# Running the FFN weights' conversion beside the first tile's normalisation, RNN and attention stages in a streaming encoder kernel

## The reference

```
h = rms_norm(x, norm_mix_g)
u, q, k, v, gl = split(h @ w_in)                      # 1024 | 1024 | 256 | 256 | 2048 columns
u = causal_dwconv(u, width 4);  y_rnn = rglru(u)      # gated linear recurrence along the frames
y_attn = banded_window_attention(rms_norm(q), rms_norm(k), v)
g_rnn, g_attn = split(sigmoid(gl + b_gate))
x = x + (g_rnn * (y_rnn @ w_rnn_proj) + g_attn * (y_attn @ w_attn_proj)) @ w_out
h2 = rms_norm(x, norm_ffn_g)
a, b = split(h2 @ w_up)                               # 2 x 2816 columns
x = x + (gelu(causal_dwconv(a, width 3)) * b) @ w_down
```

## Time and profile before

| | us |
|---|---|
| time before, median of 2 runs | 6626.67 |
| the two runs | 6571.98 and 6681.36 |
| the profiled execution's own time | 6345.69 |
| its span (slowest of 8 cores; the others from 6311.2) | 6344.1 |
| TensorE busy | 4429.2 (70% of the span) |
| VectorE, ScalarE, GpSimd busy | 2651.0, 2521.7, 330.4 |

### The profile page before, as it was taken

One profiled execution on the slowest core, in us unless ns is written; L12 is line 12 of the kernel. 1 busy time (PEld: TensorE's weight loads), 2 busy tenths in 40 slices (PEclk: granted clock), 3 DMA queues, 4 the chain that ended last, 5 costly groups with the idle time before them and its releaser, 6 DMA issues.

```text
span 6344.1 us, 81867 instructions; the slowest of 8 cores (6311.2 to 6344.1 us)
## 1 busy us (share of the span) xinstructions
PE 4429.2 (70%) x25752; PEld 2403.9 (38%) x25752; DVE 2651.0 (42%) x5630; ACT 2521.7 (40%) x4313; POOL 330.4 (5%) x446
## 2 busy tenths in 40 slices
PE   0002787878787887878787877778777878787773
PEld 0001343434444443434344443444344444444442
DVE  1002353545445353535454443535353544435353
ACT  0103444353534344444435343444445353434421
POOL 0000000000000000000000000000000000000000
PEclk9999898989898898989898989989898989899885
DMA  6775232323232423333232323233332333232335
GB/s 156 196 196 162 77 112 101 112 102 119 97 120 71 139 98 119 111 111 104 102 113 102 122 77 133 90 126 110 107 107 101 107 105 119 77 133 90 114 127 177
DMA packets 263670, 735.95 MB, mean 116 GB/s; under 512 B 22960, under 2 KB 90224, under 8 KB 263248
## 3 DMA queue, kind: packets, MB, share of 16 engines
q1 hardware_dynamic: 254480, 696.59, 33.9%
q0 software_dynamic: 8768, 34.13, 1.5%
HBM read 663.47 MB, written 67.62 MB: 115 GB/s over the span
## 4 chain that ended last, share of the span: by engine, by line
PE 54%; DMA 15%; DVE 14%; ACT 7%; issue 7%; DVEq 1%; POOL 0%; SPq 0%; ACTq 0%; POOLq 0%
PE psA L482 33%; PE psC L564 13%; DMA wsc<-yr 8%; DVE tl L530 7%; DMA ring<-wsc 6%; DVE tl L533 3%; ACT tl L522 2%; PE psA L752 1%; PE psC L836 1%; PE psB L510 1%; PE psA L818 1%; ACT xn L488 1%; DVE xn L502 1%; DVE yat L851 1%; ACT tl L658 1%
## 5 line engine op out<-in xcount | busy, mean ns | idle before, releaser
L482 PE MATMUL psA<-hTb,ring 128*128 128x512 bf16 (+1 forms) x5984 | 1301.6, 376 | 153.4 <-DVE st L536 108.6
L482 PE MATMUL psA<-hTa,ring 128*128 128x512 bf16 (+1 forms) x4624 | 1076.3, 388 | 244.8 <-DMA ring<-wsc 148.9
L530 DVE SCALAR_TENSOR_TENSOR tl<-psA,prm_s,tl 128x511 f32<-128x511 f32 (+4 forms) x1224 | 845.4, 691 | 882.9 <-ACT tl L522 468.5
L482 PEld LDWEIGHTS psA<-hTb,ring 128*128 128x128 bf16 x5984 | 561.2, 100 | 863.2 <-issue 266.5
L564 PE MATMUL psC<-ring,actb 128*128 128x256 bf16 (+1 forms) x5720 | 732.5, 290 | 209.7 <-DVE xt L571 92.8
L482 PEld LDWEIGHTS psA<-hTa,ring 128*128 128x128 bf16 x4624 | 446.1, 102 | 830.4 <-issue 407.5
L564 PEld LDWEIGHTS psC<-ring,actb 128*128 128x128 bf16 (+1 forms) x5720 | 587.1, 104 | 363.9 <-issue 234.3
L510 PE MATMUL psB<-identb,xn 128*128 128x128 bf16 (+1 forms) x1040 | 103.1, 264 | 746.7 <-DVE xn L502 736.6
L937 ACT ACTIVATE tl<-tl 128x512 f32<-128x512 f32 (+1 forms) x374 | 226.5, 606 | 930.4 <-DVE tl L533 910.5
L522 ACT ACTIVATE tl<-psA,prm_s 128x512 f32<-128x512 f32 (+1 forms) x510 | 378.7, 743 | 348.2 <-PE psA L482 332.7
L908 DVE TENSOR_TENSOR tlb<-psA,tl 128x512 bf16<-128x512 f32 (+1 forms) x136 | 90.0, 662 | 848.0 <-PE psA L482 803.4
(11 more groups left out here) (118 smaller groups left out, 4557.9 us busy)
## 6 DMA issues: line engine op xcount, KB each, us to landing
ring<-wsc SPq DMA_DIRECT2D x1020, 512.0 KB, 4.3
xt<-xp SPq DMA_DIRECT2D x16, 2048.0 KB, 8.8
yp<-xt POOLq DMA_DIRECT2D x16, 2048.0 KB, 8.7
wsc<-yr SPq DMA_DIRECT2D x110, 256.0 KB, 3.6
ring<-wsc SPq DMA_DIRECT2D x68, 384.0 KB, 3.9
actb<-w_in SPq DMA_DIRECT2D x32, 512.0 KB, 5.1
actb<-w_up SPq DMA_DIRECT2D x32, 512.0 KB, 5.0
actb<-w_down SPq DMA_DIRECT2D x22, 512.0 KB, 5.4
```

The costliest lines, as they stand in the source:

```text
L482: P.add("pe", lambda e, kc=kc: e.matmul(out_ap, lhsT=wv[:, kc, col0:col0 + 128], rhs=rhs_t[:, kc, 0:W], start=(kc == 0), stop=(kc == nk - 1)),
L530: P.add("dve", lambda e, c0=c0, L=L, s=s, wj=wj: e.scalar_tensor_tensor(out=acc[:, c0 + s:c0 + L], in0=ps[:, c0:c0 + L - s], scalar=wj, in ...
```

## The change

The 70 chunks of the FFN weights (48 of w_up, 22 of w_down) leave the prepass and become a generator, `prepass_ffn_gen`, with a yield after each chunk. It is stepped by `par` together with the first tile's stage A and front: one chunk per round. These late chunks use three f32 buffers and three bf16 buffers of their own, all in `actb`, because the front writes `yr`; the store of chunk i is recorded after the load of chunk i+2. The remaining 64 chunks keep four buffers of each kind.

The name that a store writes is no longer "wsc" for all, but ("wsc", slot) for each slot it touches, and `load_slot` reads only the name of its slot. A store still waits for the last store to the same slots, which is the one of the row block before: eight chunks back for the first 64 chunks, six back for w_up. For w_down the row block before is the chunk just ahead (`SL_DN + 3 * i + kc // 8`: eight blocks in a row go to the same four slots), so the 22 stores of w_down, but for the first of each eight, still wait for the store ahead of them.

A fence is added behind `mid` of the first tile, ahead of its `ffn_up`, which writes `actb`.

```
--- before.py
+++ after.py
@@ -294,6 +294,8 @@
     NSTG = 4
     stg_f = [actb[:, 4 * i:4 * i + 4, :].rearrange("p a b -> p (a b)").bitcast(F32) for i in range(NSTG)]
     stg_b = [yr[:, 2 * i:2 * i + 2, :].rearrange("p a b -> p (a b)") for i in range(NSTG)]
+    stg_f2 = [actb[:, 4 * i:4 * i + 4, :].rearrange("p a b -> p (a b)").bitcast(F32) for i in range(3)]
+    stg_b2 = [actb[:, 12 + 2 * i:14 + 2 * i, :].rearrange("p a b -> p (a b)") for i in range(3)]
     gstg = tl[:, 2:4, :].rearrange("p a b -> p (a b)")
 
     psA = [P.psum(f"psA{i}", [128, 512], F32) for i in range(4)]
@@ -326,8 +328,8 @@
     d_const = P.dsem("const", serial=True)
     d_x = [P.dsem("x0"), P.dsem("x1")]
     d_ring = [P.dsem(f"ring{i}") for i in range(NRING)]
-    d_stg = [P.dsem(f"stg{i}") for i in range(4)]
-    d_wst = [P.dsem(f"wst{i}") for i in range(4)]
+    d_stg = [P.dsem(f"stg{i}") for i in range(7)]
+    d_wst = [P.dsem(f"wst{i}") for i in range(7)]
     d_y = [P.dsem("y0"), P.dsem("y1")]
     d_fin = P.dsem("fin")
     d_cp = P.dsem("cp")
@@ -406,11 +408,17 @@
     pp = {"i": 0}
     _pre_ok = not (_DBG_STOP is not None and _DBG_STOP <= 1)
 
-    def prepass_chunk(src, kc, c0, ncol, dest_fn, scale):
+    def prepass_chunk(src, kc, c0, ncol, dest_fn, scale, late=False):
         i = pp["i"]
         pp["i"] += 1
-        b = i % NSTG
-        sf, sb = stg_f[b], stg_b[b]
+        if late:
+            b = NSTG + i % 3
+            sf, sb = stg_f2[i % 3], stg_b2[i % 3]
+            depth = 2
+        else:
+            b = i % NSTG
+            sf, sb = stg_f[b], stg_b[b]
+            depth = NSTG - 1
         P.dma(lambda e: e.dma_start(out=sf[:, 0:ncol], in_=src[kc * 128:(kc + 1) * 128, c0:c0 + ncol]), d_stg[b],
               writes=[("stgf", b)])
         eng = ("dve", "act", "pool")[i % 3]
@@ -432,11 +440,11 @@
         dst = wsc[s0:s0 + step * (ng - 1) + 1:step].rearrange("s p c -> p s c")[:, :, kcl * 256:(kcl + 1) * 256]
         pp.setdefault("pend", []).append(
             lambda: P.dma(lambda e: e.dma_start(out=dst, in_=sb[:, 0:ncol].rearrange("p (s c) -> p s c", s=ng)), d_wst[b],
-                          reads=[("stgb", b)], writes=["wsc"]))
-        while len(pp["pend"]) > NSTG - 1:
+                          reads=[("stgb", b)], writes=[("wsc", sl_[0]) for sl_ in slots]))
+        while len(pp["pend"]) > depth:
             pp["pend"].pop(0)()
 
-    for kc in (range(8) if _pre_ok else ()):
+    for kc in range(8):
         g = prmc(P_GM + kc, 1)
         prepass_chunk(w_in_d, kc, 0, 1024, lambda i, kc=kc: (SL_U + i, kc), g)
         prepass_chunk(w_in_d, kc, 1024, 1024, lambda i, kc=kc: (SL_Q + i, kc), g)
@@ -446,13 +454,21 @@
         prepass_chunk(wrp_d, kc, 0, 1024, lambda i, kc=kc: (SL_M + 4 * i + 0, kc), 1.0)
         prepass_chunk(wap_d, kc, 0, 1024, lambda i, kc=kc: (SL_M + 4 * i + 1, kc), 1.0)
         prepass_chunk(wout_d, kc, 0, 1024, lambda i, kc=kc: (SL_O + i, kc), 1.0)
-        gf = prmc(P_GF + kc, 1)
-        for half in range(2):
-            for (c0, ncol, p0) in ((0, 1024, 0), (1024, 1024, 4), (2048, 768, 8)):
-                prepass_chunk(wup_d, kc, half * DFF + c0, ncol,
-                              lambda i, kc=kc, half=half, p0=p0: (SL_UP + 2 * (p0 + i) + half, kc), gf)
-    for kc in (range(NFB) if _pre_ok else ()):
-        prepass_chunk(wdn_d, kc, 0, 1024, lambda i, kc=kc: (SL_DN + 3 * i + kc // 8, kc % 8), 1.0)
+
+    def prepass_ffn_gen():
+        for kc in range(8):
+            gf = prmc(P_GF + kc, 1)
+            for half in range(2):
+                for (c0, ncol, p0) in ((0, 1024, 0), (1024, 1024, 4), (2048, 768, 8)):
+                    prepass_chunk(wup_d, kc, half * DFF + c0, ncol,
+                                  lambda i, kc=kc, half=half, p0=p0: (SL_UP + 2 * (p0 + i) + half, kc), gf, late=True)
+                    yield
+        for kc in range(NFB):
+            prepass_chunk(wdn_d, kc, 0, 1024, lambda i, kc=kc: (SL_DN + 3 * i + kc // 8, kc % 8), 1.0, late=True)
+            yield
+        while pp.get("pend"):
+            pp["pend"].pop(0)()
+        yield
 
     while pp.get("pend"):
         pp["pend"].pop(0)()
@@ -470,7 +486,7 @@
         cnt["ring"] = r + 1
         ring_held[r] = True
         nv = 6 * 256 if (slot >= SL_DN and (slot - SL_DN) % 3 == 2) else 2048
-        P.dma(lambda e: e.dma_start(out=ring[:, r, 0:nv], in_=wsc[slot, :, 0:nv]), d_ring[r], reads=["wsc"],
+        P.dma(lambda e: e.dma_start(out=ring[:, r, 0:nv], in_=wsc[slot, :, 0:nv]), d_ring[r], reads=[("wsc", slot)],
               writes=[("ring", r)])
         return ring[:, r, :].rearrange("p (k c) -> p k c", k=8), ("ring", r), r
 
@@ -962,14 +978,15 @@
         return (ti, b, 32, 32, 1, [(0, 16, 1), (16, 16, 2)], False, True)
 
     load_x(0)
-    run(stageA_gen(*targs(0)))
-    run(front_gen(*targs(0)))
+    run(par([prepass_ffn_gen(), chain([stageA_gen(*targs(0)), front_gen(*targs(0))])]))
     for ti in range(NT + 1):
         b = ti % 2
         if ti + 1 <= NT:
             load_x(ti + 1)
         ta_ = targs(ti)
         mid(*ta_)
+        if ti == 0:
+            P.fence()
         gens = [ffn_up(*ta_[:6])]
         if ti + 1 <= NT:
             gens.append(stageA_gen(*targs(ti + 1)))
```

## The result

The changed kernel takes 6203.1 us (median of 11 runs, 6137.38 to 6450.26). The kernel before takes 6420.84 us in the ten runs that there are of it now (6332.54 to 6681.36). In the comparison the changed kernel's time is 0.9705 of before, 95% interval 0.9657 to 0.9754. That is 3.0% faster, 187 us of the profiled execution's 6345.7 (156 to 218 by the interval). The profiled execution of the changed kernel took 6147.0 us, 198.7 less.

A forecast was written before the change was run, and what follows sets the result against it. The prediction took the prepass stores, which all write one name and wait for each other, to set the pace. Its terms, -51 - 135 + 5 = -181 us, took 6626.7 to 6446 us; range 6285 to 6560.

The forecast's parts named there:

- Step 1: The 64 chunks staying in the prepass: stores with new names stop waiting for each other, 190 us for 241, -51 us.
- the drain: End of the early prepass: its stores must finish before the fence there, 6 us.
- Step 2: The 70 late chunks beside the first tile's stage A and front: 281 us in place of 416, -135 us.
- w_up's 164 us: The 48 late w_up chunks, with frames and ring loads in the queue: 41.9 MB at 256 GB/s, 164 us.
- the locking: Fixed-order engine lists in the late phase: chunk and front work hold each other up, DMA engines idle, +30 us.
- w_down's 73: The 22 late w_down chunks: stores to the same four slots stay chained, 3.3 us each, 73 us.
- a last attention job: End of the late phase: one attention job stands behind the last conversion on ACT, 8 us.
- Step 3: The fence behind the first tile's mid: the first ffn_up ring loads start only then, +5 us.
- The stores' chain is a symptom: Prepass and late w_up: memory gives no more than 197 GB/s however many transfers wait, 6546 us; chance 0.10.
- The queue takes more: Prepass and late w_up: mixed transfers exceed the assumed rate, 44 and 34 us more gain, 6368 us; chance 0.15.
- Half the front unhidden: First tile's front: conversions wait behind front operations, half of 127 us added instead of 30, 6480 us; chance 0.17.
- The closed loop: SP's list in the front: chunk loads, conversions, front operations and matmuls wait in a circle, slower, 6821 us; chance 0.03.

The follow-up runs named there:

- the first combined version: Changed kernel with names per slot and row block, four late buffers of each kind, and names in place of the fence: ratio to before 0.9624.
- its own experiment: Changed kernel with the fence behind mid replaced by names on the six late buffers: 233.9 us from the end of mid to the first tile's store.

## Why the prediction was right and wrong

**The change in time was right, the time was not.** Forecast were 181 us less; the ratio says 187 (156 to 218), the two profiled executions 199. The time of 6446 us and its range (6285 to 6560) missed the 6203.1 that was measured. The step that failed is the one from the profile to the median: "I carry it over as microseconds" from a profiled execution of 6345.7 to a median of two runs, 6626.7. Eight more runs of the kernel before brought that median to 6420.8, 206 us lower, so most of the miss of 243 us is the level of the two runs that were shown. The granted clock named with the result is the likely reason, but the two runs have no times by core, so this is not shown. The text said that nothing in the rows explained why those two lay 226 and 336 us above the profiled execution, and then let the range reach down only part of the way to 6165, the time it had itself worked out for an execution like the profiled one. An unexplained gap in the reference is an unknown like any other, and the range should have held both of its ends.

**Step 1** had the first frames' load near 233 us (190 for the 64 chunks, 6 for the drain). It was at 226.1 on the core of the page before and 211.9 on average. So 64 chunks took some 169 us on average, in place of 236 before (64/134 of 494): 67 us less, where 51 were forecast. The rate at full share, 256 GB/s worked out from share 0.77, was measured as 264 at share 1.06 on the page's core, and as 250 to 297 on the eight cores of the same execution from 40 to 190 us. Here are core 0 and core 5:

```profile
40.00:190.00 150.00, 0.00 (x0) 0.00 (x0) 14.12 (x20) 22.09 (x21) 20.63 (x20) 1.00 1.05 297
...
40.00:190.00 150.00, 0.00 (x0) 0.00 (x0) 11.91 (x17) 18.12 (x17) 17.28 (x17) 1.00 1.04 250
```

The reason given for 190 and not 184, that queued transfers never pack perfectly, has no row behind it: the share is 1.02 to 1.07 on all eight. The part that was taken for granted is right: SP's waits for stores are 1.6 us in the early chunks. The bound from the Trainium skill ("HBM Reference", Specifications: about 358 GB/s per core with a pair streaming) was not reached by loads and stores together: the highest rate of a stretch of 150 us here was 299. Reads alone came close to it for 14 us, and above the 323 that the prediction had as the best of its trace: core 4 of the kernel before had 350 GB/s from 540 to 554 us, at share 0.93.

```profile
40.00:190.00 150.00, 0.00 (x0) 0.00 (x0) 14.12 (x20) 21.06 (x20) 19.63 (x20) 1.00 1.07 289
```

That is the early prepass of the first combined version on the core of its page; its other cores have 287 to 299. That a chain of stores is bound by latency fits what unchaining gave: the same stores, twice as slow each, go at a higher rate once none waits for the one ahead. The Trainium skill ("DMA: Bandwidth & Descriptors", Anatomy of one DMA) puts the fixed part of a DMA issued from GpSimd down mostly to the confirmed write. These stores are issued by SP, and no run here shows what their fixed part consists of.

**Step 2** had 275 us from the first frames to mid's first matmul; on the page's core it is 263.1 (216.8 to 479.9). Of its terms, w_up's 164 us were 173 (217.2 to 389.6), with the locking that was put beside them; w_down's 73 were 68 (389.6 to 458.1); and the 8 for a last attention job were 22, since the last three stores, the 2 MB of frames and mid's first ring loads come after w_down on SP, and PE waits 9.95 us for the last of these. That wait was not in the sum, but it did not cost what it shows: with the frames' load moved away the end of mid came 2 us sooner in the combined version. The locking, +30 in the sum, comes out at 18 us by these rows (173 + 68 + 22 = 263 against 164 + 73 + 8 = 245), and the wait for the ring load is in these 18. Deeper buffers get 12 us back, and other conversion engines 11, in the same stretch. So the terms missed by 5 to 14 us each, in both directions, and step 1 by 16; that the forecast change lies within 6 us of the 187 is in part luck.

**Step 3**: the fence, +5, measured 4.2, and its own experiment gave the 4 us back.

**What the sum hid.** The forecast gives the names 51 us and the overlap 135. In the experiments names alone give 110 and overlap alone 99, and taking them out of the changed kernel costs 85 and 74. This is no contradiction (step 2's w_up chunks were costed at the unchained rate, so the names' share of them stood under overlap), but a reader of the forecast would have taken the overlap for much the larger part. It is the smaller, by 11 us.

**The rivals.** *The stores' chain is a symptom*, which had the rate capped at 197 GB/s, fell with the names alone. *The queue takes more* held in part: 250 to 297 GB/s on the cores of one execution, 259 to 299 on another chip, where 256 had been taken and 323 was its price. *Half the front unhidden* did not come about. *The closed loop* is there in small: seven waits of PE for ring loads up to mid's start, 52.6 us on the page's core, yet the DMA engines stay at 0.85 on average. In 40 slices of the 122 us of w_up beside the front their share falls to a tenth or less in four:

```profile
PE psA L498 <- DMA ring<-wsc: 52.6, 7, 9.9
```

```profile
DMA  9999998605999998105999999999498559999991
```

One number of that rival is off: 462 us for 70 chunks are 6.6 us a chunk, not 6. The phase took 263.

Of the signs of being right that were named ahead, mid's first matmul came at 480 us (near 510 forecast), the front's DMA share was 0.85 (0.7 or more), and w_down's chunks stood 3.1 us apart (3.3).

## What to carry to other kernels

A dependency kept by one name for a whole scratch tensor is a chain, and it shows as waits of the issuing queue for its own stores at a DMA share below 1; refine the name first, since here two lines gave 110 of 184 us with no overlap at all. When two things limit one phase (here a chain on one part and shallow buffers on all), try both edits together as well: here they gave at least the sum of what each gave alone. Work moved beside other work is paid for in every in-order list it passes (some 18 us here): give it enough buffers that a held conversion doesn't empty the DMA engines, and a dependency by name rather than a fence at its end.

## What the runs showed of the hardware

- Landing times doubled under load while the rate rose: a 512 KB load took 9.3 us in place of 5.0 and a 256 KB store 8.2 in place of 3.6, as the rate went from 197 to 288 GB/s and the DMA share from 0.77 to 1.05 (kernel before and names alone, the cores of their pages).
- At a full share the cores of one chip do not get the same rate: 250 to 297 GB/s in the changed kernel, 259 to 299 in its second profile (40 to 190 us), at shares of 1.02 to 1.08.
- TensorE's granted clock fell in the stretched front: 0.73 and then 0.55 with PE busy 52.65 of 122 us and 27.07 of 75 us, where the front before had 0.78 with 74.74 of 128. 0.55 is near the lower of the clock's two levels (1.2 and 2.4 GHz). What this cost was not tried; the DMA engines were at 0.85 all the while.
